# Key and value projection moved into the opening, features split in halves, and a block of zeros multiplied at the start

## The reference

```python
m_lat = split(silu(c) @ ada_w[0] + ada_b[0], 6)      # and m_ctx from c_ctx
h_lat = x_lat * (1 + m_lat[1]) + m_lat[0]            # modulate; h_ctx likewise
qa, ka, va, qb, kb, vb = split(h @ ev_w_in, [512, 640, 768, 1280, 1792])
qa, ka = rms_norm(heads(qa), q_gain), rms_norm(heads(ka), k_gain)   # 8 and 2 heads of 64
qa, ka = apply_rope(qa), apply_rope(ka)              # latent tokens only
```

## Time and profile before

| | |
|---|---|
| median of 3 runs | 1576.27 us (1574.97 to 1576.9) |
| span of the profiled execution | 1572.0 us; some 4 us of a run's time lie outside the span, and the profiled execution has no time of its own beside it |
| TensorE, VectorE, ScalarE, GpSimd busy | 98%, 68%, 56%, 21% |
| transfers | 260.35 MB, mean 166 GB/s |

### The profile page before, as it was taken

How to read it: one execution, slowest core, us unless ns; L and a number is a source line. 1 busy time by engine, 2 the same in 40 slices (tenths; PEclk the granted TensorE clock), 3 DMA queues, 4 the chain that set the end, 5 groups by cost and what they waited for, 6 DMA issues and landing times.

```text
span 1572.0 us, 25520 instructions
## 1 busy us (share of the span) xinstructions
PE 1543.6 (98%) x9936; PEld 1319.7 (84%) x9936; DVE 1067.6 (68%) x1983; ACT 880.8 (56%) x1735; POOL 337.9 (21%) x340
## 2 busy tenths in 40 slices
PE   7999999999999999999999999999999999999998
PEld 4788778988887888887999988988888898888886
DVE  4743766666444525788787768777888668779874
ACT  2423873666652423568455555756766557567662
POOL 0201420355540000112011102242221014412210
PEclk9999999999999999999999999999999999999999
DMA  9766123345657224021545562424555534335551
GB/s 369 301 238 243 21 82 134 122 182 205 236 226 261 81 108 152 13 79 68 186 177 218 184 231 105 144 104 164 187 189 187 202 142 154 139 137 188 187 202 78
DMA packets 46951, 260.35 MB, mean 166 GB/s; under 512 B 11888, under 2 KB 13168, under 8 KB 18160
## 3 DMA queue, kind: packets, MB, share of 16 engines
q1 hardware_dynamic: 43952, 252.78, 43.7%
q0 software_dynamic: 1296, 4.72, 0.8%
q10 hardware_dynamic: 1584, 1.23, 0.2%
HBM read 257.64 MB, written 1.07 MB: 165 GB/s over the span
## 4 chain that ended last, share of the span: by engine, by line
PE 90%; DVE 4%; ACT 3%; DMA 2%; issue 1%; POOL 0%; SPq 0%; DVEq 0%; ACTq 0%
PE ps L512 22%; PE ps L513 21%; PE ps L514 21%; PE ps L764 8%; PE ps L765 5%; PE ps L667 2%; PE ps L689 2%; PE ps L676 2%; PE ps L528 2%; PE ps L1164 1%; PE ps L766 1%; DMA raw<-in_ada 1%; PE ps L575 1%; DMA raw<-in_ev_w_in 1%; PE ps L1191 1%
## 5 line engine op out<-in xcount | busy, mean ns | idle before, releaser
L1931 DVE TENSOR_TENSOR wl<-raw,wh 128x1024 fp32r<-128x1024 f32 (+2 forms) x304 | 357.5, 1217 | 249.9 <-ACT wh L1437 248.6
L1437 ACT CAST wh<-raw 128x1024 fp32r<-128x1024 f32 (+1 forms) x318 | 313.6, 1036 | 337.0 <-PE ps L514 302.3
L512 PE MATMUL ps<-xx,wh 128*128 128x256 f32 (+1 forms) x1006 | 328.1, 326 | 0.0
L514 PE MATMUL ps<-xx,wl 128*128 128x256 f32 (+1 forms) x1006 | 325.5, 324 | 0.0
L513 PE MATMUL ps<-xx,wh 128*128 128x256 f32 (+1 forms) x1006 | 325.5, 324 | 0.0
L512 PE MATMUL ps<-wh,xx 128*128 128x512 f32 (+2 forms) x780 | 285.9, 367 | 2.7 <-DVE xx L2356 1.2
L514 PE MATMUL ps<-wh,xx 128*128 128x512 f32 (+2 forms) x780 | 281.1, 360 | 0.0
L513 PE MATMUL ps<-wl,xx 128*128 128x512 f32 (+2 forms) x780 | 281.0, 360 | 0.0
L2302 DVE SCALAR_TENSOR_TENSOR arena<-ps,pv,arena 128x254 f32<-128x254 f32 (+2 forms) x352 | 192.9, 548 | 28.7 <-ACT arena L1637 19.3
L512 PEld LDWEIGHTS ps<-xx,wh 128*128 128x128 f32 x1006 | 189.9, 189 | 20.1 <-issue 4.0
L514 PEld LDWEIGHTS ps<-xx,wl 128*128 128x128 f32 x1006 | 189.9, 189 | 15.2
(11 more groups left out here) (242 smaller groups left out, 2234.9 us busy)
## 6 DMA issues: line engine op xcount, KB each, us to landing
raw<-in_ada SPq DMA_DIRECT2D x46, 1024.0 KB, 5.0
raw<-in_up SPq DMA_DIRECT2D x44, 1024.0 KB, 4.9
raw<-in_fin SPq DMA_DIRECT2D x44, 1024.0 KB, 4.8
raw<-in_down SPq DMA_DIRECT2D x22, 1024.0 KB, 4.8
raw<-in_fout SPq DMA_DIRECT2D x22, 1024.0 KB, 4.8
raw<-in_win SPq DMA_DIRECT2D x12, 1024.0 KB, 4.9
raw<-in_ev_w_in SPq DMA_DIRECT2D x9, 1024.0 KB, 7.4
raw<-in_wout SPq DMA_DIRECT2D x8, 1024.0 KB, 4.9
```

What stands on the lines that cost most here:

```text
L512: e.matmul(out, A[0], B[0], start=first, stop=False)
L514: return e.matmul(out, A[1], B[0], start=False, stop=last)
L1437: e.copy(hi_of(j)[:, a:b], raw_of(j)[:, a:b]).then_inc(*S.hi.up((j, half)))
L1931: e.tensor_tensor(lo_of(j)[:, a:b], raw_of(j)[:, a:b], hi_of(j)[:, a:b].bitcast(F), ALU.subtract).then_inc(*S.lo.up((j, half)))
```

## The change

- `chunk_order`: chunk 2 of `ev_w_in` (called `KV`) is loaded right behind chunk 1, ahead of modulation chunks 3 and 7. It leaves the turns of the split chunks and has a place of its own in `HOME`. `LATER` becomes (2, 2, 3, 3, 2, 2, 2).
- TensorE: `early_kv(k)` multiplies feature k with the 256 columns of KV for four token tiles (12 matmuls of 256 columns), into halves of banks 5 and 0. It takes turns with `first` and `ada` by a new order by hand. The later `tokens` of chunk 2 is gone.
- Features are scaled, rounded and subtracted in halves of 256 tokens, each with its own signal; VectorE does feature 2n whole before 2n + 1.
- ScalarE splits KV where it split chunk 3, and chunk 3 behind feature 7. VectorE splits KV after features 4 and 5.
- GpSimd clears a block `ZERO` of 128 x 256 first, and TensorE, ahead of `ada(0, 0)`, multiplies it with itself 48 times (32 x 256 each, result unused).
- ScalarE and VectorE do tiles 0 to 3, the split of chunk 4, tiles 4 to 11, and only then the copies of qb and the splits of chunks 5 and 6. Before, the copies and splits stood after tiles 1, 3, 7 and 11.

```diff
-LATER = (2, 2, 2, 2, 2, 2, 2, 2)
+LATER = (2, 2, 3, 3, 2, 2, 2)
...
-    o = ada(0, 0, 4) + ev(0) + ada(0, 1, 5, 2, 6) + ev(1) + ada(0, 3, 7)
+    o = ada(0, 0, 4) + ev(0) + ada(0, 1, 5, 2, 6) + ev(1, 2) + ada(0, 3, 7)
     n = 8
-    for i, few in zip((3, 4, 2, 5, 6, 7), LATER):
+    for i, few in zip((3, 4, 5, 6, 7), LATER):
...
-    SPLITS = [j for j, o in enumerate(ORDER) if o[3] == "split"]
+    KV = J["ev_w_in", 2]
+    SPLITS = [j for j, o in enumerate(ORDER) if o[3] == "split" and j != KV]
...
+    KV_BANK = (5, 0)
...
+    ZERO = AR(17408, 256)
...
+        def early_kv(k, tiles=t4):
+
+            hv, lv = (v.rearrange("p (k n) -> p k n", k=8)[:, k, :] for v in (hi_of(KV), lo_of(KV)))
+            q.wait_ge(*S.hi.at((KV, k // 4)))
+            q.wait_ge(*low_done(KV, k // 4))
+            for t in tiles:
+                wait_token_feature(k, t)
+                tk = slice(128 * t, 128 * t + 128)
+                out = ps[KV_BANK[t // 2]][:, 256 * (t % 2):256 * (t % 2) + 256]
+                m = mm3(out, (xh[:, k, tk], xl[:, k, tk]), (hv, lv), k == 0 and t % 2 == 0, k == 7 and t % 2 == 1)
+                if k == 7 and t % 2:
+                    m.then_inc(*S.proj.up(("kv", t - 1), ("kv", t), ("use", KV)))
+
+        q.wait_ge(*S.gps.at("zero"))
+        for n in range(48):
+            g = n % 4
+            e.matmul(ps[0][32 * g:32 * g + 32, 0:256], ZERO[:, 0:32], ZERO, start=True, stop=True)
         ada(0, 0)
         ada(0, 1)
         ada_finish(0)
...
         first(0)
         ada(1, 0)
+        first(1, (0,))
         ada(1, 1)
-        first(1, (0, 1))
+        first(1, (1,))
         ada_finish(1)
         first(1, (2, 3))
         ada(2, 0)
         first(2, (0, 1))
         ada(2, 1)
-        first(2, (2, 3))
+        first(2, (2,))
         ada_finish(2)
-        first(3)
+        first(2, (3,))
+        for k in (3, 4, 5):
+            first(k)
+        early_kv(0)
         ada(3, 0)
-        first(4, (0, 1))
+        early_kv(1)
         ada(3, 1)
-        first(4, (2, 3))
+        early_kv(2, (0,))
         ada_finish(3)
-        for k in (5, 6, 7):
+        early_kv(2, (1, 2, 3))
+        for k in (3, 4, 5):
+            early_kv(k)
+        for k in (6, 7):
             first(k)
+        for k in (6, 7):
+            early_kv(k)
...
-        ada_few()
-        bs = tokens("ev_w_in", 2, "kv", t4, turns=False)
-        for t in t4:
-            free[bs[t]] = [(S.ea, ("va", t))]
...
         for k in range(8):
-            q.wait_ge(*S.vec.at(("feat", "f0", k)))
-            e.copy(xh[:, k, :], tmp[:, k % 2, :]).then_inc(*S.xh.up(("f0", k)))
+            for g in range(2):
+                w = slice(256 * g, 256 * g + 256)
+                q.wait_ge(*S.vec.at(("feat", "f0", k, g)))
+                e.copy(xh[:, k, w], tmp[:, k % 2, w]).then_inc(*S.xh.up(("f0", k, g), ("f0", k)))
...
             if k in (3, 5):
-                weights(SPLITS[k // 2])
+                weights(SPLITS[1] if k == 3 else KV)
+        weights(SPLITS[2])
...
-        for tile in QK[0:2]:
+        for tile in QK[0:4]:
             qk(tile)
         weights(after(J["ev_w_in", 1]))
-        for tile in QK[2:4]:
+        for tile in QK[4:12]:
             qk(tile)
         copies_qb(copy, 0)
         weights(after(J["ev_w_in", 3]))
-        for tile in QK[4:8]:
-            qk(tile)
         copies_qb(copy, 1)
         weights(after(J["ev_w_in", 4]))
-        for tile in QK[8:12]:
-            qk(tile)
-        weights(after(J["ev_w_in", 2]))
...
             if n == 2:
                 weights_half(SPLITS[1], 0)
-            for k in (2 * n, 2 * n + 1):
-                feature_low(k)
+            feature_low(2 * n)
+            feature(2 * n + 1)
+            feature_low(2 * n + 1)
             if n == 2:
                 weights_half(SPLITS[1], 1)
+                weights(KV)
...
+        e.memset(ZERO, 0.0).then_inc(*S.gps.up("zero"))
```

## The result

The changed kernel takes 1583.88 us, median of 6 runs (1582.04 to 1589.27), beside 1576.59 for the kernel before in the same session (6 runs, 1574.97 to 1581.22). The quotient of these medians is 1.0046; the ratio on record, which is not that quotient, is 1.0054, 95% interval 1.0041 to 1.0066. Slower by half a per cent, and inside the range. In the three later sessions the kernel before has medians of 1573.91, 1574.0 and 1573.92, so that from here on each kernel stands against runs of the kernel before in its own session, on the same chip. One execution of the kernel before, 2173.1 us at a granted clock of 0.66, is a slow one and enters no ratio. Run again so, the changed kernel takes 1582.52 (ratio 1.0054, 1.0042 to 1.0067), profiled span 1581.0.

A forecast was written before the change was run, and what follows sets the result against it. TensorE, busy 98%, was taken as the bound, so only its idle time and rate count. A late split (+6.2 us, opening included) and the clock (+1.7) gave +7.9: span 1579.9, time 1584.2 us, range 1577.5 to 1588.

The forecast's parts named there:

- The 4.3 us between span and time: Whole kernel: the runs' median 1576.27 lies 4.3 us above the span, so span 1579.9 becomes 1584.2.
- The opening: TensorE up to 57.75: feature 4 starts at 31.85 instead of 33.52, early key and value work follows; worth 1.84 us.
- The list ahead of the tiles: VectorE's fixed work before the tiles gets longer: positions at 50.2 instead of 45.60, first tile's sum at 56.0 instead of 51.38.
- The tiles: VectorE's twelve tiles: 39.6 us less 6.0 of removed splits and copies plus 1.9 of returning waits, 35.5 us.
- The wait: Ahead of ev 5's block TensorE asks at 86.5, gets the split at 94.5: +6.2 us, bounds +0.2 and +8.2.
- The clock: After the mid-kernel wait of some 6.5 us TensorE runs at the slow rate: +1.7 us, bounds 0 and 2.2.
- The zeros: 48 products at TensorE's start end at 9.0 and speed the first modulation chunks: taken as 0, bounds -0.3 and +2.
- The other side: Rival: the tile chain ends before TensorE asks at 86.5, leaving only the opening's 1.84 us gain: 1574.4 us, chance 0.09.

The follow-up runs named there:

- both mends: Changed kernel with qb 0's copy and chunk 5's split between tiles 7 and 8, and the angle table computed ahead of group 3: 1572.55 us (0.9991), again 1572.63 (0.9993).
- the fill: Changed kernel plus 15 products with unused result on TensorE ahead of the block of chunk 5: 1582.29 us (1.0053), again 1582.81 (1.0055).
- 16 zeros: The kernel with both mends, with 16 products of zeros at the start instead of 48: 1571.55 us, ratio 0.9985 (0.9976 to 0.9994).

## Why the prediction was right

It said 1584.2 us, +7.9 on the kernel before. The kernel took 1583.88, which is 7.3 us above the kernel before in the first session and 8.6 and 9.1 in the two later ones. The mechanism was right: VectorE's list of tiles delays the split of chunk 5, TensorE waits for it, and the clock falls. That the two times agree to 0.3 us is luck in part. The 4.3 us between span and time were taken from a median and another execution's span; in the later sessions a profiled execution's time is 1.3 to 1.5 us above its own span. And the parts of the sum measure 9.1 us in the second session, not 7.9.

- **The opening.** Feature 4 was to start at 31.85; it starts at 32.31. The gap that had been at 33.52 is gone. ScalarE casts chunk 1 from 29.40, not from 28.95, which is the 0.45 us. The key and value work ended at 57.98, predicted 57.75. The price of 1.84 us for the opening shows only once nothing eats it: at the milestone of 113.34 the kernels with both mends are 1.5 and 0.4 us ahead with 48 zeros, and 2.0 without zeros and with 16 of them.
- **The list ahead of the tiles.** Positions were predicted at 50.2, the first sum at 56.0. They came at 50.67 and 56.45, the same 0.45 us late. The 5.8 us between them, taken over from the earlier trace rows, held.
- **The tiles.** 35.5 us from the first sum to the end of the last tile, from which 6.0 us were taken for what had left the list and to which 1.9 us came back. From 56.45 to the copy at 92.07 it is 35.6. VectorE's waits for ScalarE grew from 6.0 us in 8 to 7.6 in 10: they did take up what the splits had filled, 1.6 us of the predicted 1.9. The row at 90.75 still waits 0.67 us.
- **The wait.** Predicted: wanted at 86.5, had at 94.5, 1.6 us of it earlier for a bank. Measured: wanted at 88.1 (86.7 without the 1.34 us for the bank), had at 95.12, 7.05 idle. By the prediction's own sum 95.12 + 0.93 - 89.27 = +6.8, not +6.2.
- **The clock.** Predicted +1.7, bounds 0 and 2.2. In the block itself 2.3 us, just outside, and 1.5. With 6.8 that makes 9.1, and the modulation chunks of 113.34 stand at 122.31, 9.0 later. The two pairs with the fill put TensorE 1.4 (1.8 less the earlier opening) and 1.5 us ahead at 145 us, near the predicted 1.7; for the whole kernel the medians show 0.4 us, give or take 1, so that there the term looks too large. That the modulation chunks land just when asked for held with the fall (no wait at 108.48). Without it they are asked for earlier and the last is 0.6 us late, which the prediction didn't set against the price of the clock. By the Trainium skill, TensorE: Matmul & The Clock Gate, Part 1, activity releases the slow rate and idleness brings it back. By that rule the trace agrees: 0.50 behind 7.05 us without work, 1.00 behind a wait filled with products.
- **The zeros.** They ended at 8.1 (9.35 at the latest of all profiles), predicted 9.0, and were priced at nothing, bounds -0.3 and +2. Nothing measured contradicts that price, but its working fails. By its own rates 4 us at the slow rate and the rest at the fast one end at 9.7, not 9.0, and the 96 records took 6.98 to 8.25 us, which by the same rates is between no slow part at all and some 3 us of it (an estimate). And nothing in it has the first weights land later (in seven of ten profiles), which TensorE then waits for.
- **The other side.** The rival in which the chain ends before TensorE asks, with 1.84 us to gain, is what the kernel with the split moved builds. Its ratio, 1.0002, lacks the gain: a bank is still waited for (1.34 us), and in its profile the first weights came late. With both mends the medians are 1.3 and 1.4 us below, with 16 zeros 2.4. So the rival's price was fair. What was named against it held too: the waits of up to 0.9 us for ScalarE stand in the mended kernels as well. The split was moved ahead of four tiles, the loop was not made faster.

## What to carry to other kernels

When work moves forward on one engine, look at what stands ahead of each of its operands in the other engines' own lists: here a split of 2.35 us, four tiles too far back in a list in program order, cost 8 us and hid a gain of up to 2. The measured length of a chain, with its waits in it and only whole instructions taken out or put in, forecast its end to about 0.5 us. Work that depends on nothing but an early transfer belongs into the idle time ahead of the chain, not at its head.

## What the runs showed of the hardware

The clock doesn't fall by the length of a wait alone. In the seven profiles with late first weights TensorE waited 2.0 to 2.5 us ahead of its first product. In four of them the level fell behind it (waits of 2.21, 2.02, 2.12 and 2.38 us), in three it didn't (2.40, 2.46 and 2.33). TensorE's timeline of the changed kernel, first session, shows the fall:

```profile
15.38 0.76 PE L516 MATMUL ps<-wh,xx 128*128 128x512 f32 x1 [2.21 <-ACT wh L1483]
```

against 0.47 us for the same record at 15.27 in the second session; from 15.2 to 18.2 the granted clock is 0.50 in the one and 1.00 in the other. A wait that is safe in one execution isn't in the next. Even without zeros two kernels with the same opening differ: the 26 records of unused products ahead of the first feature took 1.91 us in the changed kernel without zeros and 3.62 in the one with both mends. The prediction had taken 1.7 us as the longest harmless wait. The Trainium skill, TensorE: Matmul & The Clock Gate, Part 1, has the moments at which activity is judged run on their own, whatever the kernel does; the mixed outcome agrees with that, and no run here proves it.

The granted clock of a stretch can read 1.00 where records run at half rate: before the change it did so over the first 32 records, 3.66 us where 1.94 is the fast time. Here, at the start of the program, the durations tell the rate and the column doesn't.
